# A hybrid decoder step on one core: queries and keys of the prompt attention split into fp16 parts when evicted, turned by transposing DMAs, and scored in three fp16 terms

## The reference

```python
def hybrid_layer(x, C0, n0, m0, S0, k_buf, v_buf, pos0, ...):
    u = rms_norm(x, norm_gain)
    (mq, mk, mv, mo, mz, mi, mf, rq, rk, rv, rz, aq, ak, av, az) = split(u @ w_in)
    out_m = head_norm(sigmoid(mo) * mlstm(mq, mk, mv, mi, mf)) * silu(mz)      # 4 heads of 64
    out_r = head_norm(retention(rope(rq), rope(rk), rv)) * silu(rz)            # 4 heads of 64
    h_a = window_attention(aq, ak, av, k_buf, v_buf, ...)                      # 8 query, 2 key/value heads
    out_a = h_a * silu(az)
    return x + concat(out_m, out_r, out_a) @ w_out

# window_attention: every query sees the 128 positions up to its own
s = einsum('bnqhgd,bnkhd->bnhgqk', qb, kb) * HEAD_DIM ** -0.5 + bias
m = max(max(s), sink);  p = exp(s - m);  denom = sum(p) + exp(sink - m)
o = einsum('bnhgqk,bnkhd->bnqhgd', p / denom, vb)
```

## Time and profile before

| | us |
|---|---|
| median of 3 runs | 2067.92 |
| lowest, highest | 2067.12, 2072.01 |
| span of the profiled execution, first to last instruction | 2062.8 |
| median of the runs less that span | 5.1 |
| PE, DVE, ACT, POOL busy in the span | 2001.7, 1654.9, 883.6, 333.2 |

### The profile page before, as it was taken

The page is one execution under the profiler, slowest core; times in us unless marked ns, Lnnn a source line. Parts: engine busy times, 40 slices in busy tenths (PEclk is TensorE's granted clock), DMA queues, the critical chain, the costliest instruction groups (busy, mean ns, idle before and its releaser), DMA issues.

```text
span 2062.8 us, 36194 instructions
## 1 busy us (share of the span) xinstructions
PE 2001.7 (97%) x12814; PEld 1126.3 (55%) x12814; DVE 1654.9 (80%) x3968; ACT 883.6 (43%) x2246; POOL 333.2 (16%) x320
## 2 busy tenths in 40 slices
PE   6999999999999999999989999999999999999998
PEld 3555555555555555545455555555555555554453
DVE  7788888888888888675566888888888888888766
ACT  7744444444444446231265444444444444462100
POOL 2011111111111212120010111111111111111200
PEclk9999999999999999999999999999999999999999
DMA  9221111122111123885630122111121111258552
GB/s 330 45 35 51 46 42 42 42 54 50 42 42 42 43 53 123 202 235 153 207 136 21 43 50 56 42 42 42 42 52 43 42 52 43 77 150 191 141 131 94
DMA packets 255811, 173.66 MB, mean 84 GB/s; under 512 B 216135, under 2 KB 229384, under 8 KB 255564
## 3 DMA queue, kind: packets, MB, share of 16 engines
q1 hardware_dynamic: 239732, 140.91, 26.9%
q0 software_dynamic: 7424, 29.43, 4.0%
q10 hardware_dynamic: 8568, 2.18, 0.5%
HBM read 85.29 MB, written 41.06 MB: 61 GB/s over the span
## 4 chain that ended last, share of the span: by engine, by line
PE 86%; DVE 8%; ACT 2%; DMA 2%; issue 1%; DVEq 0%; SPq 0%; ACTq 0%
PE J L581 53%; PE J L1298 13%; PE W L987 3%; PE W L998 2%; DVE W L572 2%; PE W L1070 2%; PE W L1100 1%; PE W L1088 1%; PE W L1059 1%; PE T L1079 1%; PE W L973 1%; PE J L1034 1%; ACT W L565 1%; DMA ST<-ST 1%; PE W L1005 1%
## 5 line engine op out<-in xcount | busy, mean ns | idle before, releaser
L581 PE MATMUL J<-W,uT_mix 128*128 128x512 f16 (+2 forms) x3072 | 609.5, 355 | 2.0 <-issue 1.7
L581 PE MATMUL J<-W,x_mix 128*128 128x512 f16 (+2 forms) x3072 | 607.1, 354 | 2.0 <-issue 2.0
L581 PEld LDWEIGHTS J<-W,uT_mix 128*128 128x128 f16 x3072 | 298.7, 99 | 272.9 <-issue 11.5
L581 PEld LDWEIGHTS J<-W,x_mix 128*128 128x128 f16 x3072 | 297.9, 98 | 271.6 <-issue 10.7
L1418 ACT ACTIVATE PB<-J,out_scale 128x512 f32<-128x512 f32 (+2 forms) x256 | 154.5, 603 | 305.3 <-PE J L581 297.0
L1388 ACT ACTIVATE ST<-ST,small 128x1024 f16<-128x1024 f32 x32 | 36.7, 1148 | 205.7 <-DVE small L1897 205.7
L1298 PE MATMUL J<-W,EM_qkR_mix 128*128 128x512 f16 x480 | 115.3, 379 | 0.0
L2350 POOL TENSOR_TENSOR ST<-ST,ge 128x512 f32<-128x512 f32 x32 | 67.8, 2118 | 218.2 <-DVE ST L1881 218.2
L1298 PE MATMUL J<-W,x_mix 128*128 128x512 f16 x400 | 99.1, 387 | 0.0
L1382 ACT ACTIVATE sc_xr<-sc_xr,small 128x128 f32<-128x128 f32 x256 | 98.6, 390 | 0.0
L1298 PE MATMUL J<-W,uT_mix 128*128 128x512 f16 x400 | 97.6, 383 | 0.0
(11 more groups left out here) (472 smaller groups left out, 3500.2 us busy)
## 6 DMA issues: line engine op xcount, KB each, us to landing
W<-in_w_in POOLq DMA_DIRECT2D x8, 2048.0 KB, 10.4
mix_d<-ST SPq DMA_DIRECT2D x32, 512.0 KB, 2.6
sc_xr<-in_x_prompt SPq DMA_DIRECT2D x20, 512.0 KB, 4.2
sc_xr<-x SPq DMA_DIRECT2D x20, 512.0 KB, 3.8
ST<-in_w_in POOLq DMA_DIRECT2D x4, 2048.0 KB, 12.3
W<-in_w_out SPq DMA_DIRECT2D x4, 2048.0 KB, 8.1
PB<-in_x_prompt SPq DMA_DIRECT2D x6, 512.0 KB, 3.7
x<-PB SPq DMA_DIRECT2D x6, 512.0 KB, 3.5
```

What stands on the lines that cost most here:

```text
L581: mm = nc.tensor.matmul(out, stationary(k, a), moving[:, k, b, :], start=(k == 0 and n == 0), stop=(k == KT - 1 and n == 2))
```

## The change

Queries and keys are no longer transposed by PE. At eviction ACT writes the high fp16 part of the queries straight from PSUM into `q_rows` (which takes the place of the fp32 queries in PB), and DVE the low part (`q_lo`) from the same bank; the keys' parts are made from PB, on ACT in `v_hi` and on DVE in `v_lo`, into `k_rows`. SP turns both by transposing DMAs (`turn_keys`, 128 by 256 numbers of fp16; `turn_queries`, 128 by 1024) into `kT16` and `qT16`. `kT16` has a slot for odd and one for even chunks, so nothing is moved for the next chunk; the slots change sides, and DVE's `scores` picks them by `odd`. PE's `scores` is 24 fp16 matmuls instead of 8 of fp32. Power-of-two scales keep the parts in the range of fp16, and `qk_scale` takes them out. The rope table is loaded in two halves. `part_s` moves from qTA to HH, so the waits for the stored projections go from ACT to DVE (`kept`). PE's block after aq on the same bank waits for `q_lo`. On ACT the eviction of aq moves ahead of `mix_hi`; on DVE `v_lo` and `q_lo` stand ahead of `mix_size`.

```diff
--- before.py
+++ after.py
...
-        kTA = sb("kTA", [P, 2 * P])
+        kT16 = sb("kT16", [P, 2, 2, P], F16)
+        k_rows = sb("k_rows", [P, 2, P], F16)
+        qk_scale = sb("qk_scale", [P, 1])
...
-        qTA = qTA_part[:].rearrange("p (k t) -> p k t", k=4)
+        oTA = qTA_part[:].rearrange("p (k t) -> p k t", k=4)
+        qT16 = qTA_part[:].bitcast(F16).rearrange("p (s k t) -> p s k t", s=2, k=4)
+        q_rows = PB[:, AQ:AK].bitcast(F16).rearrange("p (s c) -> p s c", s=2)
...
-        part_s = [qTA_part[:, 256 * i:256 * i + 256] for i in range(2)]
+        part_s = [HH_all[:, 256 * i:256 * i + 256] for i in range(2)]
...
             V.tensor_scalar(out_scale[:, i:i + 1], wm[:, 1:2], 2.0 ** -14 / U_SCALE, None, ALU.mult)
+            if SAMPLE_ORDER[j] == "aq":
+                V.tensor_scalar(qk_scale[:], wm[:, 1:2], out_scale[:, IDX["akv"]:IDX["akv"] + 1],
+                                2.0 ** -14 / U_SCALE * V_SCALE ** -2 * QK_SCALE, ALU.mult, ALU.mult)
...
+        def load_rope(sp, rows, part):
+            cols = slice(HD * part, HD * part + HD)
+            sp.dma_start(ropet[:, cols], A["rope"][rows, cols]).then_inc(E["rope_loaded"], 16)
+
+        def turn_keys(sp, odd):
+            sp.dma_start_transpose(kT16[:, odd], k_rows[:].rearrange("p s c -> p (s c)")).then_inc(E["kT_loaded"], 16)
+
+        def turn_queries(sp):
+            sp.dma_start_transpose(qT16.rearrange("p s k t -> p (s k) t"), q_rows.rearrange("p s c -> p (s c)")
+                                   ).then_inc(E["qT_loaded"], 16)
+
...
-            def next_rope(n, c, turning):
-                this, after_row = keep(sp, n + 2 if turning else n + 1), keep(sp, (c + 1) * CHUNK)
-                sp.wait_ge(E["uT_ready" if turning else "rope_ready"], this)
-                sp.dma_start(ropet[:], A["rope"][bass.ds(after_row, CHUNK), :]).then_inc(E["rope_loaded"], 16)
+            def next_rope(n, c, part):
+
+                this, after_row = keep(sp, n + 1 if part else n + 2), keep(sp, (c + 1) * CHUNK)
+                sp.wait_ge(E["q_lo" if part else "uT_ready"], this)
+                load_rope(sp, bass.ds(after_row, CHUNK), part)
...
+                if p == 6:
+                    sp.wait_ge(E["k_lo"], N0 + 1)
+                    turn_keys(sp, 0)
+                    sp.wait_ge(E["q_lo"], N0 + 1)
+                    wait(sp, E["o_psum"], N0)
+                    turn_queries(sp)
                 if layer == 0 and p == 6:
                     load_bias(sp)
-            next_rope(N0, 0, False)
+            sp.wait_ge(E["rope_ready"], N0 + 1)
+            for part in range(2):
+                load_rope(sp, slice(CHUNK, 2 * CHUNK), part)
 
...
                     turn_probs(sp)
-                    next_rope(n, c, True)
+                    next_rope(n, c, 0)
                     turn_next(odd)
+                    next_rope(n, c, 1)
+                    turn_keys(sp, odd)
+                    turn_queries(sp)
                 else:
...
             load_residual(0)
+            sp.wait_ge(E["q_lo"], NE)
+            turn_keys(sp, 1)
+            turn_queries(sp)
...
-            def keys(n):
-
-                pe.wait_ge(E["proj_evac"], NBLK * n - 1)
+            def scores(n, attn, odd):
+
                 wait(pe, E["o_read"], n - 1)
                 pe.wait_ge(E["rqk_ready"], n)
-                pe.wait_ge(E["wR_ready"], n)
+                pe.wait_ge(E["r_out_read"], n)
+                pe.wait_ge(E["kT_loaded"], keep(pe, 16 * n))
+                pe.wait_ge(E["qT_loaded"], keep(pe, 16 * n))
+                slots_of = slice(1 - odd, 2 - odd) if attn == "first" else slice(0, 2)
+                terms = ((0, 0), (0, 1), (1, 0))
                 for t in range(4):
-                    TR(B[0][:, t * P:(t + 1) * P], PB[:, AQ + t * P:AQ + (t + 1) * P], ident)
-                TR(B[1][:, 0:P], PB[:, AK:AK + P], ident).then_inc(E["aqk_psum"], 1)
-
-            def scores(n, attn):
-
-                pe.wait_ge(E["qA_ready"], n)
-                pe.wait_ge(E["kA_ready"], n)
-                pe.wait_ge(E["r_out_read"], n)
-                if attn == "full":
-                    pe.wait_ge(E["kprev_ready"], n - 1)
-                lo = P if attn == "first" else 0
-                for t in range(4):
-                    for kv in range(A_KV):
-                        bank = W03[:, 1024:2048] if kv == 0 else W03[:, 0:1024]
-                        mm = MM(bank[:, t * 256 + lo:t * 256 + 256], qTA[64 * kv:64 * kv + 64, t, :],
-                                kTA[64 * kv:64 * kv + 64, lo:256], start=True, stop=True)
-                        if t == 3:
-                            mm.then_inc(E["scores_psum"], 1)
+                    for i, (a, b) in enumerate(terms):
+                        for kv in range(A_KV):
+                            bank = W03[:, 1024:2048] if kv == 0 else W03[:, 0:1024]
+                            out = bank[:, t * 256:t * 256 + 256].rearrange("p (o c) -> p o c", o=2)
+                            mm = MM(out[:, slots_of, :], qT16[64 * kv:64 * kv + 64, a, t, :],
+                                    kT16[64 * kv:64 * kv + 64, slots_of, b, :], start=(i == 0), stop=(i == 2))
+                            if t == 3 and i == 2:
+                                mm.then_inc(E["scores_psum"], 1)
 
...
 
             def project_block(n, b, odd):
                 i = IDX[b]
                 uT = uT_of(layer, odd)
                 w = BLOCK[b][1] - BLOCK[b][0]
                 wait(pe, E["proj_evac"], NBLK * n + i - 1)
+                if b == "gates":
+                    pe.wait_ge(E["q_lo"], keep(pe, n))
                 pair_products(J[i % 2][:, 0:w], lambda k, s: uT[:, s, k, :], pair[b]).then_inc(E["proj_done"], 1)
 
             def first_block(p, bank):
...
+                if p == 5:
+                    pe.wait_ge(E["q_lo"], n + 1)
...
             def unit(n, c, odd, attn, more):
-                keys(n)
                 if attn == "first":
                     pe.wait_ge(E["uT_ready"], n + 1)
                 else:
                     pe.wait_ge(uT_loaded, keep(pe, 16 * ((CHUNKS - 2) * layer + c - 1)))
                 project_block(n, "gates", odd)
-                scores(n, attn)
+                scores(n, attn, odd)
                 project_block(n, "mqk", odd)
                 pe.wait_ge(E["proj_evac"], NBLK * n + 1)
...
                         pe.wait_ge(E["proj_evac"], NBLK * NE - 1 + n)
+                        pe.wait_ge(E["q_lo"], NE)
...
 
-                    cp(PB[:, lo:hi].rearrange("p (t k d) -> p k t d", t=4, k=2),
-                       src.rearrange("p (k t d) -> p k t d", t=4, k=2)).then_inc(E["proj_evac"], 1)
+                    af(q_rows[:, 0].rearrange("p (t k d) -> p k t d", t=4, k=2),
+                       src.rearrange("p (k t d) -> p k t d", t=4, k=2), ACT.Copy, scale=V_SCALE
+                       ).then_inc(E["proj_evac"], 1)
...
                 act.wait_ge(E["proj_evac"], evacuated)
+                af(k_rows[:, 0], PB[:, AK:AK + P], ACT.Copy, scale=v_scale[:, 0:1])
                 af(v16[:, odd, 0, :], PB[:, AV:AV + P], ACT.Copy, scale=v_scale[:, 0:1]).then_inc(E["v_hi"], 1)
...
                 gate_exp(n)
-                if attn == "first":
-                    for i in range(2):
-                        act.wait_ge(kept[i], 32 * (NBLK // 2) * (layer + 1))
-                queries(n)
                 act.wait_ge(E["gates_m"], n)
...
                     next_hi(n)
+                    evac(n, "aq")
                     mix_hi(n)
-                    evac(n, "aq")
                     gate_first(n, "r")
...
-            def keys(n, attn):
-                dve.wait_ge(E["aqk_psum"], n)
-                if attn == "full":
-                    dve.wait_ge(E["kprev_ready"], n - 1)
-                V.tensor_copy(kTA[:, P:2 * P], B[1][:, 0:P]).then_inc(E["kA_ready"], 1)
-
...
-            def scores(n, attn):
+            def scores(n, attn, odd):
                 c_attn.begin(dve, n - 1)
+                cur, earlier = (slice(P * i, P * i + P) for i in (1 - odd, odd))
                 past = const("past").bitcast(I32).unsqueeze(1).to_broadcast([P, 4, WINDOW])
                 for kv in range(A_KV):
                     dve.wait_ge(E["scores_psum"], 2 * n - 1 + kv)
                     bank = heads(W03[:, 1024:2048] if kv == 0 else W03[:, 0:1024])
-                    before = neg.unsqueeze(1).to_broadcast([P, 4, WINDOW]) if attn == "first" else bank[:, :, 0:P]
+                    before = neg.unsqueeze(1).to_broadcast([P, 4, WINDOW]) if attn == "first" else bank[:, :, earlier]
                     V.memset(small_p[:, 113:114], 0.0)
-                    at(V.copy_predicated(bank[:, :, P:], past, before))
-                    V.scalar_tensor_tensor(sc[:, 4 * kv:4 * kv + 4, :], bank[:, :, P:], QK_SCALE,
+                    at(V.copy_predicated(bank[:, :, cur], past, before))
+                    V.scalar_tensor_tensor(sc[:, 4 * kv:4 * kv + 4, :], bank[:, :, cur], qk_scale[:],
```

(45 more changed lines are left out.)

35 lines of the change are left out of this document (13 added, 22 removed).

## The result

The changed kernel takes 2042.66 us (median of 4 runs, 2041.86 to 2044.35), the kernel before 2068.99 (4 runs beside it); the ratio is 0.9875, 95% interval 0.9855 to 0.9894. So it is faster by 26.3 us, of the 33.1 that I forecast. The time lies 7.7 us above the forecast of 2035 and inside its range of 2028 to 2054.

The account below looks back on a forecast made before the run. PE alone was taken to bound the full chunks: 30 x 1.11 = 33.3, + 1.2 - 1.2 - 0.2 = 33.1 us off the 2062.8 span gives 2029.7; plus 5.1, 2035 us, range 2028 to 2054 (8 in 10).

Parts of the forecast that it names:

- The mechanism that the forecast rests on: Full chunks: PE alone bounds; no transposes gains 0.58 us, fp16 scores in overlapping row halves 0.53, period 46.83.
- the forecast itself: Whole kernel: the forecast with its own spread in scores, prologue and stores, 2030 to 2041 us, chance 0.62.
- rival A: Full chunks: DVE becomes the bound if a new operation meets POOL's; 2060 us, or 2045 at half; chance 0.24.
- Rival B: Scores on PE: fp16 row halves don't overlap, so scores take 2.73 us; 2076 us, chance 0.06.
- a wait of 0.3 us for r_out: Full chunks: DVE ends the gate inverse at 440.3 and waits 0.3 us for PE's r_out at 440.6.
- slack 0.2: Full chunks: DVE waits 0.3 us at r_out but lags another 0.1 through the chunk, leaving 0.2 us.
- both rows that I had: Transposing DMAs of the kernel before: u_rows lands in 4.3 us (median), the probabilities, behind a load, in 5.5.
- the 2.5 us to spare: SP's transposes: 5.1 us for issues and landing, of the 7.6 us between q_lo and the scores.
- Rival C: SP's queue between q_lo and the scores: late transposes hold PE, 2075 to 2141 us; chance 0.08.
- 1.2 of cost and 0.2 of gain: Layer 0's start: q_lo 0.82, keys' high half and scalar add about 0.4; DVE loses L1809, 0.20 on the chain.
- 1.11 for each way to a layer's last scores: Output stages: the full chunk's PE gain, 0.58 net for transposes plus 0.53 for scores, again in each layer.
- Output stages: the same 1.11 each: Layers' ends: each output stage's attention gains as a full chunk does, 1.11 us; layer 1's prologue steps change nothing.

Follow-up runs that it names:

- the run that takes the overlap away: Changed kernel with the key heads in the outer loop, 12 score matmuls on one row half, then 12 on the other: 2065.16 us.
- the run with one term: Changed kernel with only the high fp16 halves multiplied in the scores, 8 matmuls in place of 24: 2037.62 us.
- six loads in front: Changed kernel with six small loads on SP's queue in each chunk, ahead of the key and query transposes: 2057.73 us.
- the early rope: POOL's sample rope moved ahead of its wait for the mix store between the layers: kernel before 2061.85 us, changed kernel 2032.07 us.

## Why the prediction was right, and where it fell short

The mechanism that the forecast rests on came true, and the sum fell 7 us short at the layers' ends. The measured 2042.66 us lies outside the 2030 to 2041 that I gave the forecast itself, and inside the range only by the part that I had kept for rival A. Rival A did not come, so that the range held is in part luck.

- **PE in the full chunks: right, term by term.** The scores took 1.42 us for 1.40; the gates block behind half-array work took 2.81, 0.11 more than its like, so the transposes were worth 0.58 net. The period came out at 46.84 for 46.83. The 28 chunk-to-chunk steps gave 29.4 us, 26 full ones of 1.10 and two that start at a first chunk, of 0.34 and 0.44. Rival B is refuted by the 1.42 us, and the run that takes the overlap away shows that the overlap is the reason.
- **The Trainium skill's rule on weight loads** ("TensorE: Matmul & The Clock Gate", LDWEIGHTS) would give the estimated 2.56 us for 24 loads in series. The trace has 1.42 with the halves in turns, and 2.31 even without, so here the measurement decides against that sum.
- **DVE: in time, with more room than I said.** I forecast a wait of 0.3 us for r_out and measured 0.67; DVE's timeline of the changed kernel has the reason:

```profile
429.33 0.34 DVE L2038 SCALAR_TENSOR_TENSOR k_rows<-PB,v_scale,k_rows 128x128 f16<-128x128 f32 x1
...
430.52 1.20 DVE L1907 TENSOR_REDUCE small<-ST 128x1 f32<-128x1024 f32 x1
```

  From the start of the keys' low half to that of `mix_size` it is 1.19 us for the low halves of keys, values and queries, where I had 1.50: I added up durations, and consecutive operations overlap, so that from start to start they cost less. Of these 0.31 us 0.16 are lost again, as `m_gated` starts that much later against r_out. ACT's `mix_hi` steps 1.05 us for 1.15 in the same way. The rest, some 0.1, I have not traced. No new operation in the chunks met POOL at a doubled price, so rival A did not come there. But the "slack 0.2" that I named for DVE's lag through the chunk is, by the run with one term, 0.18 of another kind: PE cannot shorten the scores by more than that.
- **The transfers: right in the sum, by two errors that cancel.** They landed 2.3 and 3.2 us after issue, below both rows that I had (4.3 taken). But SP spent 0.72 us on rope's second half and 1.17 on the keys before it issued the queries, where I had 0.34 and 0.5. So the 2.5 us to spare are as forecast by luck; six loads in front use them up. Rival C did not come.
- **First chunks and layer 0's prologue: the cost right, the gain half there.** Up to layer 0's first scores the change lost 1.2 us, where I had 1.2 of cost and 0.2 of gain; traces of the same code differ by 1 us and more in this stretch (the kernel before with the early rope took 111.0 us up to there), so this is no close check. The step from the first to the second scores should have gained 0.39 by the first scores and 0.58 by the next transposes; it gained 0.34 in layer 0 (46.54 to 46.20) and 0.44 in layer 1 (46.54 to 46.10), 1.2 us short for both. PE's timeline of the changed kernel, in the first chunk of layer 0:

```profile
128.75 0.40 PE L1080 MATMUL T<-thirds,k 96*128 96x128 bf16 x4 [0.47 <-ACT qkM_wo L1486]
```

  PE waits there for ACT, 0.47 us in layer 0 and 0.37 in layer 1; the kernel before doesn't wait. It is the wait that the run with one term brings into every chunk. In a first chunk DVE is the last to start, as the prediction itself said, so the round through DVE and ACT is the limit, and shorter PE work doesn't shorten it. The run with the key heads one after the other agrees: its first scores take 1.29 us in place of 0.84, the wait is gone and the step is the same 46.21. So 0.84 of the 1.2 us are these waits and 0.14 the first scores, which took 0.84 for 0.77 us each; the rest I have not traced.
- **The last units: half wrong.** I counted 1.11 for each way to a layer's last scores, less 0.2 for both. They gained 0.8 and 0.5. In layer 1 PE waits 0.44 us for r_weights, which I left behind q_lo and a block of w_out without pricing its reader there; with it moved ahead the stretch is 0.7 shorter. Short by 0.8 in all.
- **Between the layers: wrong, and this is the step that failed.** I forecast nothing but the saved scores there ("Output stages: the same 1.11 each", layer 1's prologue "nothing"), some 0.7 us of gain. The traces show 4.0 of loss. I had followed SP, ACT and DVE through a full chunk, and never asked what stands on POOL's queue behind the wait for the last mix store; its reader's wait of 0.62 us in the one trace looked harmless. With the rope early the kernel before gains some 6 us and the changed one some 10, and the stage differs by 0.9 between them. So the wait is a cost that both kernels had, and its length hangs on whether POOL's rope meets DVE's two operations on 64x1280 numbers, a doubled price such as I had feared in rival A, but for old instructions and in another stage. How much of the 4.7 us the change itself causes, and how much is the luck of four traces (one block at half clock is 2.6 us), stays open.
- **The time around the span: harmless, but not what I called it.** I added 5.1 us, the median less the span of the profiled execution. Wherever an execution's own time stands beside its span, it is 1.8 or 1.9 us longer (2042.47 and 2040.6; 2070.29 and 2068.5). The other 3 us were scatter: the profiled execution was a quick one among runs from 2061 to 2075 us. As a saving was taken off the median, the forecast didn't suffer, but spans alone (2062.8 to 2040.6) would have shown a gain of 22.2, four too few.

The sum by the two pairs of traces: 33.1 forecast, 24.9 measured, 8.2 short. Of that 4.7 lie between the layers, 1.2 in the first steps, 0.2 in the 26 full ones, 0.8 in the last units, 0.2 in the prologue and 1.1 behind the last scores. There PE's idle time is the same in both kernels within 0.4 us, so what differs is clock and scatter.

## What to carry to other kernels

Where every engine runs a queue in order, look in the stages between the loops at what is queued behind each wait without needing it; the wait that matters there may cost nothing in the one trace that you have and several microseconds in the next. The idle time in front of one wait prices only work added at that place: what another engine may shed is set by the next round of waits, here 0.18 us against 0.67. Where a step starts with another engine already late, as in the first chunks here, that round is the limit from the start. And small matmuls on half of the array's rows should take turns between the halves: 24 of 256 columns cost 1.42 us so, and 2.31 one half after the other.

## What I had not expected of the hardware

- Half-array fp16 matmuls one after the other on the same half (64 rows, 256 columns, each with its own load of 128 columns) take 0.096 us each, less than the 0.114 of a full one of 256 columns (2.73 / 24).
- The time of a transposing DMA from SBUF to SBUF grew far less than its size: 2.3 us for 128x256 fp16, 3.2 for 128x1024, 4.3 for 128x2048. Their issue takes SP 1.2 and 1.3 us. That of a load of 128 single values takes 0.47.
- On POOL a tensor_tensor of 64x512 took 1.26 us, and 2.39 or 2.47 where DVE's L2871 or L2872 (64x1280 each) ran beside it; one of 64x256 took 0.72, and 1.8 to 2.1.
- The same block of matmuls, behind the same 2.02 us of idleness, ran at the full granted clock in one execution and near half of it in another, 2.9 against 5.4 us. A saving in a stage where PE often stands can't be read from one trace.
